# One block for a layer's norms, rope, products, compression and stick-breaking heads, and length factors in a delta-rule block

## The reference, cut to what matters

```
q = l2_normalize(q) * (GDN_HEAD_DIM ** -0.5)          # t * rsqrt(sum(t*t) + EPS), 8 heads of 128
k = l2_normalize(k)
o_gdn = rms_norm(o_fw + o_bw, gdn_norm_w) * silu(g_gate)
```

```
q = (rmsnorm(c_q, q_norm) @ w_uq)       # 6 heads of 64 + 32; the 32 are roped
kv = (rmsnorm(c_kv, kv_norm) @ w_ukv)   # keys and values of 64 each; k_rope is roped
q, k_cmp, k_sel, k_win = (rope(t, pos, PARTIAL_ROT) for t in ...)
kc = gelu(flat(blocks(k_cmp) + pos) @ w1) @ w2        # the same for v_cmp
# stick breaking, 4 heads of 64:
z = q @ k * scale
log_beta, log_rem = log_sigmoid(z), where(strict, log_sigmoid(-z), 0)
suffix = cumsum(log_rem, reverse=True) - log_rem
a = where(strict, exp(log_beta + suffix), 0);  out = a @ v
```

## Time and profile before

| | |
|---|---|
| median of 3 runs | 4170.15 us (4169.01 to 4175.66) |
| the profiled execution's own time | 4174.96 us, its span 4173.2 us |
| busy in the span | PE 82%, PEld 58%, DVE 44%, ACT 25%, POOL 6% |
| mean granted PE clock | 0.908 of full |
| delta-rule stage | about 84 to 765 us of the span |
| rope stage to compress, per layer | 109.5 us, from 2169.79 and again from 3418.93 |
| the two stick-breaking stages, per layer | 70.8 us, from 2395.35 |
| route stage, DVE's ranking | 1211.51 to 1246.14 us |
| DMA of a slab of 1024 KB of `w_mix` | 5.2 us from issue to landing (median) |
| DMA of `w_router`, 64 KB | 1.8 us |

### The profile page before, as it was taken

The page is one execution under the profiler, slowest core; times in us unless marked ns, Lnnn a source line. Parts: engine busy times, 40 slices in busy tenths (PEclk is TensorE's granted clock), DMA queues, the critical chain, the costliest instruction groups (busy, mean ns, idle before and its releaser), DMA issues. The chain is left out here.

```text
span 4173.2 us, 39560 instructions
## 1 busy us (share of the span) xinstructions
PE 3427.7 (82%) x15206; PEld 2418.9 (58%) x15206; DVE 1828.3 (44%) x2595; ACT 1062.6 (25%) x1607; POOL 269.8 (6%) x230
## 2 busy tenths in 40 slices
PE   4787986768768776999785859998999785869997
PEld 3463755433553223888662547886888563447886
DVE  2778676455541002442324644433442324644433
ACT  2121222121321002222211643222222211643222
POOL 1100101010110001000111000000000111000001
PEclk7899998989879998999896979999999896989998
DMA  2100000100203990222111012222222111012221
GB/s 80 41 31 31 21 11 1 51 38 13 81 1 151 420 396 31 101 101 91 71 46 51 1 41 101 90 101 76 97 101 94 68 46 51 1 41 101 94 98 60
DMA packets 49249, 325.07 MB, mean 78 GB/s; under 512 B 6880, under 2 KB 7264, under 8 KB 11104
## 3 DMA queue, kind: packets, MB, share of 16 engines
q1 hardware_dynamic: 49120, 323.34, 20.7%
HBM read 320.17 MB, written 2.10 MB: 77 GB/s over the span
## 5 line engine op out<-in xcount | busy, mean ns | idle before, releaser
L358 PE MATMUL psum<-ffn_x_hi,ffn_w_hi 128*128 128x512 f32 x1408 | 551.7, 392 | 13.8 <-DVE ffn_x_lo L314 13.8
L358 PE MATMUL psum<-ffn_x_lo,ffn_w_hi 128*128 128x512 f32 x1408 | 550.9, 391 | 0.0
L358 PE MATMUL psum<-ffn_x_hi,ffn_w_lo 128*128 128x512 f32 x1408 | 550.5, 391 | 0.0
L303 DVE TENSOR_TENSOR ffn_w_lo<-ffn_raw,ffn_w_hi 128x2048 fp32r<-128x2048 f32 x128 | 293.4, 2292 | 421.1 <-ACT ffn_w_hi L274 421.1
L104 PE MATMUL psum<-mix_normed,mix_ring 128*128 128x512 f32 x832 | 374.4, 611 | 81.7 <-DVE recurrences_work L624 39.3
L274 ACT ACTIVATE ffn_w_hi<-ffn_raw 128x2048 fp32r<-128x2048 f32 x128 | 245.2, 1916 | 572.9 <-PE psum L358 572.5
L104 PEld LDWEIGHTS psum<-mix_normed,mix_ring 128*128 128x128 f32 x832 | 162.6, 197 | 290.2 <-issue 248.0
L358 PEld LDWEIGHTS psum<-ffn_x_hi,ffn_w_hi 128*128 128x128 f32 x1408 | 266.3, 189 | 75.5 <-DVE ffn_w_lo L310 20.0
L358 PEld LDWEIGHTS psum<-ffn_x_hi,ffn_w_lo 128*128 128x128 f32 x1408 | 266.2, 189 | 55.8
L358 PEld LDWEIGHTS psum<-ffn_x_lo,ffn_w_hi 128*128 128x128 f32 x1408 | 266.5, 189 | 55.2
L358 PE MATMUL psum<-ffn_hid_hi,ffn_w_hi 128*128 (+1 forms) x704 | 273.9, 389 | 0.0
(11 more groups left out here) (425 smaller groups left out, 5382.2 us busy)
## 6 DMA issues: line engine op xcount, KB each, us to landing
ffn_raw<-w_ffn SPq DMA_DIRECT2D x128, 1024.0 KB, 4.8
mix_ring<-w_experts SPq DMA_DIRECT2D x48, 1024.0 KB, 13.8
mix_ring<-w_mix SPq DMA_DIRECT2D x38, 1024.0 KB, 5.2
mix_normed<-w_experts SPq DMA_DIRECT2D x24, 1024.0 KB, 14.8
experts_work<-w_experts SPq DMA_DIRECT2D x24, 1024.0 KB, 15.7
mix_ring<-w_gdn SPq DMA_DIRECT2D x16, 1024.0 KB, 4.8
mix_ring<-w_ssd SPq DMA_DIRECT2D x10, 1024.0 KB, 6.8
mix_ring<-w_out SPq DMA_DIRECT2D x8, 1024.0 KB, 5.6
```

The lines of the kernel that those rows point to most:

```text
L303: dve.tensor_tensor(w_lo[:, q, :], raw[:, q, :], w_hi[:, q, :].bitcast(F32), ALU.subtract)\
L358: ins = pe.matmul(out, wp[:, q, w], xp, start=start and a == 0, stop=stop and a == 2)
```

## The change

In `gdn_heads`, queries are not normalised any more: the output's own norm takes their length out, if EPS is scaled by it. So ACT keeps the squares of q (times EPS x 128 x 128) in `q_sq`, which borrows the memory of the rope tables, and `out` adds them to the output's sum by one more matmul per head. Keys stay unscaled too: eight matmuls with one column of ones sum their squares per token into 8 columns (`k_rows`), and the reciprocal root multiplies `beta`, `beta_decay` and `to_end` (`by_key`) and the decay mask. The gates go straight into `m.mixed`. `low_levels` is split in two, with conv(p, 0) between them; `out_scale` moves between the levels of the inverse. The route stage loads the rope tables again.

In the second block, eight stages become one, `heads_front`, ahead of attention. All small products pass through PSUM banks 6 and 7 in turn (`order`; `free` waits for the reader of the product before last), the sticks' logits lie in banks 0 to 5, all 1280 columns of a head together, and each pass over them is one instruction. `S_Q` is scaled when projected, the latent norms' lengths are taken per token and spread by a diagonal, GELU uses Exp in place of Tanh, and the weight slabs load from the stage's start.

```diff
@@ gdn_heads
+    q_sq = cut(m.rope_tables, 0, 2, 2, T)
+    k_rows = cut(m.cur_buf, 0, 2, NT)
@@ POOL
-                pool.wait_ge(normed, 4 * p + 4)
+                pool.wait_ge(summed, p + 1)
...
+                pool.wait_ge(k_done, 3 * p + 3)
@@ PE: lengths, out, inverse, loop
-                for n in range(4):
-                    pe.wait_ge(squared, 4 * p + n + 1)
-                    pe.matmul(m.ps[:, 4 + n, :], m.ones, flat(sq[:, n, :, :]), start=True, stop=True)\
-                        .then_inc(summed, 1)
+                for hh in range(2):
+                    pe.wait_ge(squared, 2 * p + hh + 1)
+                    for t in range(NT):
+                        at = hh * NT + t
+                        ins = pe.matmul(m.ps[:, 4, at:at + 1], k_sq[:, hh, t, :], m.ones[:, 0:1], start=True,
+                                        stop=True)
+                ins.then_inc(summed, 1)
...
+                    pe.matmul(m.ps[:, 6 + hh, :], m.ones, q_sq[:, q % 2, hh, :], start=True, stop=False)
+                    pe.matmul(m.ps[:, 6 + hh, :], m.ones, back[hh], start=False, stop=True).then_inc(o_summed, 1)
...
-                    pe.wait_ge(shifted, 4 * (q + 2))
+                    pe.wait_ge(shifted, q + 2)
+                    if q:
+                        pe.wait_ge(o_shifted, 2 * q)
...
-                        if n == 5:
-                            lengths(p)
+                    lengths(p)
@@ DVE
+            def keys(p):
+                dve.wait_ge(summed, p + 1)
+                dve.tensor_scalar(k_rows, m.ps[:, 4, 0:2 * NT].rearrange("p (h t) -> p h t", h=2), EPS, None,
+                                  ALU.add).then_inc(shifted, 1)
+                dve.wait_ge(rooted, p + 1)
+                link(dve.reciprocal(k_rows, k_rows))
+                for n, dst in by_key.items():
+                    dve.tensor_tensor(dst, m.scal[n][:, :, :, 2 * p:2 * p + 2], by_row, ALU.mult)\
+                        .then_inc(k_done, 1)
...
-                    if q + 1 < pairs:
-                        scale(q + 1, l - 4)
+                    if q and l < 6:
+                        out_scale(q - 1, (l - 4,))
...
-                    dve.tensor_tensor(dec[:, i, :, :], dec[:, i, :, :],
-                                      upto[d].unsqueeze(1).to_broadcast([P, NT, P]), ALU.mult)\
-                        .then_inc(masked, 1)
+                    for t in range(NT):
+                        ins = dve.scalar_tensor_tensor(dec[:, i, t, :], dec[:, i, t, :], k_rows[:, hh, t:t + 1],
+                                                       upto[d], ALU.mult, ALU.mult)
+                    ins.then_inc(masked, 1)
...
-                    low_levels(p - 1)
-                if p >= 2:
-                    out_shift(p - 2)
+                    invert_lanes(p - 1)
                 if p < pairs:
                     conv(p, 0)
-                if p >= 2:
-                    out_scale(p - 2)
+                if p:
+                    lay_blocks(p - 1)
                 if p < pairs:
                     conv(p, 2)
                     conv(p, 4)
-                    shift(p)
...
+                    keys(p)
+                if p >= 2:
+                    out_shift(p - 2)
@@ heads_front: PE's queue
+            scores(0)
...
+            turn("kc")
+            spread("spread_q", 0)
+            spread("spread_kv", 1)
+            turn("k_pe")
+            mla_q(0)
+            mla_q(1)
...
+            ins.then_inc(hidden_done, 1)
+            suffix(0, 0)
+            turn("ks")
+            suffix(0, 1)
+            turn("kw")
...
+            mla_q(2)
+            mla_q(3)
...
+            turn("q0")
+            values(0)
+            scores(1)
+            mla_q(4)
+            mla_q(5)
+            for name in ("rq0", "rq1", "q1", "q2"):
+                turn(name)
...
+            suffix(1, 0)
+            turn("rq2")
+            suffix(1, 1)
+            for name in ("rq3", "rq4", "rq5"):
+                turn(name)
+            values(1)
@@ heads_front: DVE, one head of a stick pair
+                    dve.scalar_tensor_tensor(beta(e), logits(e), 0.0, beta(e), ALU.min, ALU.subtract)\
+                        .then_inc(betas, 1)
...
+                    dve.tensor_tensor(rem(e), beta(e), logits(e), ALU.subtract).then_inc(rems, 1)
...
+                dve.tensor_tensor(beta(e), beta(e), logits(e), ALU.add).then_inc(added, 1)
@@ heads_front: DVE's queue behind compression
+            add(0, 0)
+            rope("ks")
...
+            add(0, 1)
+            mask(0, 0)
+            rope("kw")
+            mask(0, 1)
...
+            rope("q0")
+            put(0)
+            for name in ("rq0", "rq1", "q1", "q2"):
+                rope(name)
+            sticks_in(1)
+            for t in range(NT):
+                dve.wait_ge(projected, mla_count[f"mla_v{t}"])
+                dve.tensor_copy(b.v_mla[:, t, :], ps(f"mla_v{t}")[:, 0:MLA_H * HD]).then_inc(v_copied, 1)
+            add(1, 0)
+            rope("rq2")
+            add(1, 1)
+            rope("rq3")
+            mask(1, 0)
+            mask(1, 1)
+            rope("rq4")
+            rope("rq5")
+            put(1)
@@ heads2
+    heads_front(nc, m, b, slabs, turned)
     attention(nc, m, b, turned)
-    for pair in range(SB_H // 2):
-        stick_breaking(nc, m, b, pair, turned)
```

More of the change, by code:

```diff
@@ L1807, in _ @@
                     .then_inc(read_v, 1)
-def rope_stage(nc, m, name, tiles, tmp, after=None):
-    with stage(nc, m, name) as (block, sem):
-        turned, read, scaled, chain, done, swapped = sem(6)
-        @block.tensor
-        def _(pe):
-            for n, (x, turn, _, _) in enumerate(tiles):
-                if n >= 4:
-                    pe.wait_ge(read, n - 3)
-                rows = x.shape[0]
-                pe.matmul(m.ps[0:rows, n % 4, :], turn[0:rows, 0:rows], x, start=True, stop=True)\
-                    .then_inc(turned, 1)
+STICK_AT = {0: 0, 1: T, 3: T + (NT - 1) * P, 2: 2 * T}
@@ new lines, in add, with mask, put @@
+            def add(pair, e):
+                dve.wait_ge(suffixed, 2 * pair + e + 1)
+                dve.tensor_tensor(beta(e), beta(e), logits(e), ALU.add).then_inc(added, 1)
+            def mask(pair, e):
+                dve.wait_ge(beta_exped, 2 * pair + e + 1)
+                mask_own(e, 0, masked)
+            def put(pair):
+                dve.wait_ge(valued, pair + 1)
+                dve.tensor_copy(turned[:, head_dst + pair, :], ps(f"values{pair}")).then_inc(stored, 1)
+            dve.wait_ge(cleared, 4)
@@ new lines, in _ @@
+            blocks(1, N_VC, "pos_v")
+            dve.wait_ge(summed, 1)
+            for n, width in ((0, 2 * P), (1, P)):
+                dve.tensor_scalar(lengths[:, n, :], ps("sums")[:, n * NT:(n + 1) * NT], 1.0 / width, EPS, ALU.mult,
+                                  ALU.add).then_inc(mean, 1)
+            dve.wait_ge(rooted, 1)
+            dve.reciprocal(lengths, lengths).then_inc(inverted, 1)
+            dve.wait_ge(inverted, 1)
+            for n in range(2):
+                dve.tensor_tensor(diagonal[:, n, :, :], m.ident.unsqueeze(1).to_broadcast([P, NT, P]),
+                                  lengths[:, n, :].unsqueeze(2).to_broadcast([P, NT, P]), ALU.mult).then_inc(laid, 1)
```

565 lines of the change are left out of this document (313 added, 252 removed).

## The result

The changed kernel takes **3963.0 us** (median of four runs, 3962.19 to 3973.03) where the kernel before takes 4172.31 (median of four, 4169.01 to 4175.66): the ratio is 0.9504, with a 95% interval of 0.9486 to 0.9521. The forecast was 3965. The profiled execution took 3963.0 with a span of 3961.1, against 4174.96 and 4173.2 before.

What follows compares the result with a forecast made beforehand. The touched stretches were taken as bound by waiting between engines. Gains of 163 us (heads and attention, two layers) and 42 (delta-rule block) sum to 205: 3970 from the profiled 4174.96, a median of 3965, range 3925 to 4028.

Steps and rivals of the forecast that it cites:

- First pair: Delta-rule block: wide reciprocals and their multiplications go, so PE starts the decay products sooner; gain 20.3 us (18.5 and 22).
- Mask step: Delta-rule block: sixteen 128-wide instructions instead of four 512-wide ones, 1.8 us later on DVE in four pairs; loss 7.2 us.
- Second pair: Delta-rule block: laying the inverse's blocks moves behind conv(0), so the inverse begins sooner; gain 6.6 us, 9.2 without slow restart.
- Third and fourth: Delta-rule block: inverse starts 12.9 us sooner in each pair, 25.8 in all; out_scale between the inverse's levels loses 2.4.
- End of the block: Delta-rule block behind the fourth pair: out_scale changes places with equal work, the last output sum comes 0.9 us later.
- The reload: Route stage: reloading the rope tables (1.18 MB) is hidden beside DVE's ranking; would cost 5 us if not.
- Heads block: Per layer, the new single stage takes 101 us instead of 180.3 by a walk of the queues; gain 79.3 us.
- Attention: Behind the heads block: attention's first records may start warm, worth 2 us per layer.
- (a): Rival: small waits hold the clock down, the heads block takes 125 us, the kernel 4018; chance 0.20.
- (b): Rival: the hand-written order of the heads block doesn't overlap, 35 us saved per layer, the kernel 4058; chance 0.08.
- (d): Rival: PE's clock stays at the lower level through heads block (160 us) and attention, the kernel 4248; chance 0.02.
- (c): Rival: queues overlap better, the heads block takes 90 us, the kernel 3934; chance 0.12.

Runs made afterwards that it cites:

- delta_only: Changed kernel's new delta-rule block, with its reload of the rope tables, and the eight old stages of the heads: 4135.6 us, 0.9916 of the kernel before.
- mask_wide: Changed kernel with the mask step as four 512-wide products, the keys' factor of the scores left out: 3957.5 us, 0.9490 of the kernel before.
- more_banks: Changed kernel with five small products of the heads block in banks of the first stick head instead of banks 6 and 7: 3973.3 us, 0.9524.
- best: Changed kernel with the mended delta-rule block, more banks and DVE's new order in the heads block, and the filled pause: 3935.7 us, 0.9431.
- banks_and_order: Changed kernel with five small products in other banks and, on DVE, masks and the copy of hidden units reordered in the heads block: 3951.0 us, 0.9477.

## Why the prediction was right

**First pair (20.3).** Measured 23.0 to the first `kb`. The mechanism is the predicted one: the lengths took 1.84 for my 2, POOL's product followed in 1.27 for my 1.2. PE began the decay products 1.2 us sooner in the period than I had it, and from there to `kb` it is 1.5 less, as the clock stayed up here: in `delta_only` and five others the first decay product took 2.05 us and the first period 76.4 to 78.0, a gain of 18.7 to 20.3. With the 2.05 of the earlier trace rows the term is right; the extra 2.7 are luck.

**Mask step (-7.2).** 4.28 us for my 16 x 0.26; 1.8 per pair on DVE, shown. Worth about half in the end, by one trace.

**Second pair (6.6).** With the mask step 4.8 for the period; measured 5.3. The slow restart that I took at 2.6 is there: tiles 6 and 7 took 16.28 instead of 13.9.

**Third and fourth (25.8, less 2.4 and two mask steps).** 19.8 by my terms; measured 8.6 + 9.7 = 18.3. I had the inverse start behind the output's shift, and it did; the restart behind that wait (5.60 us instead of the 3.81 of the earlier trace rows, at a granted 0.66) was not in the sum. It is 1.8 and 1.4 (5.25 us) in the two pairs, more than the missing 1.5, so something else gave a little back; I don't know what.

**End of the block.** By my terms 2.7 us more, measured 4.4. Sum of the block: forecast 42, measured 42.2, with errors of 2.7, 0.5, -1.5 and -1.7 that cancel.

**The reload.** Hidden, as said.

**Heads block (79.3 per layer).** 101 us said, 101.24 and 97.85 measured. The sums of the engines hold too: PE 83.12 for 82, DVE 64.91 for 64, ACT 36 for 38, POOL 27 for 28. The walk's marks fall behind slowly. Scores and sums end at 6.9 (said 7.0), the second query product at 22.1 (19.0), compression at 30.2 (29.0), the query products of heads 2 and 3 at 49.2 (46.0), scores(1) at 55.9 (54.2), sticks_in(1) start at 69.5 (66.6), the second suffix ends at 88.1 (86.3), the last values at 99.5 (93.9). Each of the three jumps holds a slow restart behind a wait of 3 to 4 us: 1.8 at the second query product, 1.7 at heads 2 and 3, 2.0 at the last values. These are 5.5 where I had put a lump of 3 at the end, and a fourth, 0.9 at the turn behind 3.11 us of waiting, comes on top; the 2.4 for hand-overs covered most of the rest. Scores(1) at 2.43 rather than the cautious 4.0 gave 1.6 back, and compression took 8.2 for 10.1. So the sum is right by errors that cancel, and the long waits are where the walk has them. No run divides the gain among the seams, the loads that are now hidden and the wide passes over the logits: that split is argued.

**The rule on POOL and DVE.** I put the stretch at 1.03 on every rope add and by the Trainium skill's rule ("GPSIMD Engine Reference", Specifications), that VectorE instructions with two SBUF inputs contend with GpSimd, other steps would stretch too. They do: masks of 384 columns take 1.18 us beside POOL's copies of `k_pe` and 0.55 alone, and one add took 2.89. A mean per add hid that: most rope adds took 0.69, and the price is the length of POOL's work that happens to run, not a factor.

**Attention (2 per layer).** 2.8 in layer one. Its first four records take 2.38 us for 3.68, so about half of the gain is the warmer start.

**Rivals.** (a) the lower clock: 0.87 and 0.90 were granted, where 0.75 would have decided for it; PE was busy for 82% of the block. The Trainium skill ("TensorE: Matmul & The Clock Gate", A second HAM failure mode) tells of a kernel with banks passed in turn whose clock goes down and up between bursts. The trace agrees in kind, with slow restarts behind the 3 us waits, and puts the price at some 6 us per block and not the 24 of (a). (b) and (d) have nothing for them. (c) is what the improved order approaches: 92 to 95 us for its 90. PE's waits in the block come to 18 us in all, below my 25.

**What I left out.** In stretches of unchanged work, 2.8 us of gain between the mixers and 2.3 lost in the first ssd group; and layer two's block, which was 3.4 shorter than layer one's. The 2.8, and perhaps part of layer two's 86.7, belong to the execution of the kernel before that was profiled: `delta_only`, which leaves the mixers as they were, gains 2.8 and 8.7 in the same two stretches. That the whole landed within 2 us is partly luck. The spans differ by 212.1 us where I had 205; and I took off 4.8 for the offset from profiled to median time, while the changed kernel's profiled execution is its median.

## What to carry to other kernels

Walk the queues in order and price every stop of PE twice, as the wait and as the slow products behind it, and ask which chain a wait is slack of before spending banks on it: here DVE's order, on top of the banks, was worth 5.0 and 3.3 us in the two layers, and the banks alone 1.5 and 0.8. Read an edit's worth from the stretch that it touches, and look at the stretches that it doesn't: here these moved by as much as most edits were worth. Where engines pass work to each other, count what POOL's products cost the DVE steps that others wait for; moving four of them to DVE made DVE's run 0.8 us shorter and the block no faster.

## What the runs showed of the hardware

- **The same instructions, another clock.** Twelve kernels are alike up to the first `kb`: in the six where PE's first decay product, behind an idle time of 1.27 us, took 1.10 us this period is 73.3 to 74.3 us, in the six where it took 2.05 it is 76.4 to 78.0. The granted clock of that product is 1.00 in the changed kernel and 0.50 in `delta_only`. The first ssd group took between 162.19 and 168.24 us with nothing of its own changed. Medians of kernels with edits in one stage can't be compared closer than that.
- **The same attention ran at several levels of the mean clock**: 624 records took 107.7 to 108.9 us at a granted 0.97 to 0.98 behind scores and values that didn't share the array, 113.2 at 0.92 behind most blocks where they did, but there also 110.03 at 0.95 (`mask_wide`, layer two) and 114.7 to 114.8 at 0.91 (`more_banks`, layer one; `best`, layer two). What sets that level I didn't find out.
- **Two fp32 products in opposite halves** of the array overlap: eight score products (16 records) in 2.43 us in turns, 4.03 apart.
- **A DVE instruction with both inputs in SBUF stops for POOL**: the add took 2.89 us for 0.69, through the rest of one product of POOL and all of the next. In the tail of `banks_and_order` three masks and three products of POOL went on by turns, 4.0 us for masks that take 1.4 alone, and POOL's middle product took 1.59 us for 1.28. Products of DVE that read PSUM (L2110, 0.69) ran beside POOL at their own price.
- **One-column products**: eight (16 records) in 1.84 us. PE's next 32 records take 5.35 to 6.73 us behind them and a 2 us wait, 3.81 behind them and 0.46 us.
